# A four-phase decoder trunk: second-layer weights in row-wide pieces, waits for one head's routing, three value slots on VectorE while a chunk is mixed, and the first chunk alone ahead of the first gather

## The reference, cut to what matters

```python
def peer(xn, w_q, sub_keys, u_tab, v_tab):
    q = (xt @ w_q).reshape(t, PEER_HEADS, 2, PEER_HALF)
    s = jnp.einsum("thpd,hpnd->thpn", q, sub_keys)
    # two top-16 lists per head, their 256 sums, top 16 of these -> idx, softmax g
    u = jnp.take(u_tab, ic, axis=0)
    a = jnp.einsum("cd,chkd->chk", xc, u)
    w = gc * jax.nn.gelu(a, approximate=False)
    vv = jnp.take(v_tab, ic, axis=0)
    return jnp.einsum("chk,chkd->cd", w, vv)
```

## Time and profile before

| | |
|---|---|
| median of 3 runs | 1624.27 us |
| the profiled execution's own time | 1625.22 us |
| its span, first to last instruction | 1623.3 us |
| busy share PE / DVE / ACT / POOL | 83% / 66% / 29% / 62% |
| bytes moved, mean rate | 617.13 MB, 380 GB/s |
| of these gathers / SP's transfers | 536.94 MB / 79.26 MB |
| PE's granted clock, mean | 0.91 of 2.4 GHz |

### The profile page before, as it was taken

How to read it: one execution, slowest core, us unless ns; L and a number is a source line. 1 busy time by engine, 2 the same in 40 slices (tenths; PEclk the granted TensorE clock), 3 DMA queues, 4 the chain that set the end, 5 groups by cost and what they waited for, 6 DMA issues and landing times.

```text
span 1623.3 us, 17094 instructions
## 1 busy us (share of the span) xinstructions
PE 1339.6 (83%) x4558; PEld 769.0 (47%) x4558; DVE 1073.2 (66%) x2529; ACT 468.5 (29%) x1427; POOL 1013.6 (62%) x1099
## 2 busy tenths in 40 slices
PE   7999798888895899888777799989877978777775
PEld 7887544444552564354343376546444433322222
DVE  4248689988775545637787635664877977755555
ACT  0203333333332222432233221441333322211112
POOL 0006677777547655766666745675777677777774
PEclk9999999999997998899989899999988989888887
DMA  9519999999999999999999999999999999999997
GB/s 335 180 57 369 397 396 409 404 405 405 393 389 365 399 391 394 407 406 390 400 402 403 410 392 387 402 392 367 408 401 404 409 410 409 409 409 409 410 409 274
DMA packets 222153, 617.13 MB, mean 380 GB/s; under 512 B 18881, under 2 KB 88571, under 8 KB 222075
## 3 DMA queue, kind: packets, MB, share of 16 engines
q0 software_dynamic: 147456, 536.94, 84.0%
q1 hardware_dynamic: 74619, 79.26, 14.7%
HBM read 615.07 MB, written 1.05 MB: 380 GB/s over the span
## 4 chain that ended last, share of the span: by engine, by line
PE 33%; DMA 20%; POOL 15%; issue 13%; DVE 11%; ACT 6%; POOLq 0%; SPq 0%; DVEq 0%; ACTq 0%
DMA u_ring<-in_peer_u_dram,idx_now 18%; PE acc L807 16%; PE tile L777 13%; POOL v_ring L532 8%; POOL u_ring L532 7%; DVE u_ring L1022 5%; ACT diag L622 2%; ACT gelus L616 2%; DMA v_ring<-in_peer_v_dram,idx_now 2%; PE tile L909 1%; PE xf L777 1%; PE tile L904 1%; DVE xres L1049 0%; ACT pq L718 0%; PE tile L799 0%
## 5 line engine op out<-in xcount | busy, mean ns | idle before, releaser
L807 PE MATMUL acc<-v_ring,diag 128*128 128x512 f32 x1780 | 864.7, 644 | 117.7 <-ACT diag L622 64.8
L1022 DVE CUSTOM_DVE_ANT_0 u_ring<-u_ring,xf 128x1024 f32<-128x1024 f32 x512 | 613.5, 1215 | 275.3 <-DMA u_ring<-in_peer_u_dram,idx_now 273.0
L532 POOL DMA_INDIRECT v_ring<-in_peer_v_dram,idx_now x512 | 497.1, 971 | 291.8 <-PE acc L807 119.8
L807 PEld LDWEIGHTS acc<-v_ring,diag 128*128 128x128 f32 x1780 | 363.0, 209 | 589.3 <-issue 550.6
L532 POOL DMA_INDIRECT u_ring<-in_peer_u_dram,idx_now x512 | 501.2, 979 | 168.7 <-issue 138.9
L608 ACT ACTIVATE gelus<-dots 128x8 f32<-128x8 f32 x64 | 13.4, 209 | 526.4 <-DVE dots L1022 526.4
L622 ACT ACTIVATE diag<-ident,gelus 128x128 f32<-128x128 f32 x448 | 137.8, 388 | 2.1
L777 PE MATMUL tile<-w_ring,fT 128*128 128x256 f32 x480 | 110.3, 383 | 3.7 <-DVE fT L1171 3.7
L777 PEld LDWEIGHTS tile<-w_ring,fT 128*128 128x128 f32 x480 | 92.1, 193 | 27.4 <-issue 12.0
L616 ACT ACTIVATE gelus<-gelus,gates 128x1 f32<-128x1 f32 x512 | 102.1, 281 | 4.1 <-ACT gelus L608 2.3
L726 ACT ACTIVATE gexp<-best,gstat 128x16 f32<-128x16 f32 x32 | 9.8, 307 | 308.3 <-DVE best L1312 308.3
(11 more groups left out here) (170 smaller groups left out, 1046.1 us busy)
## 6 DMA issues: line engine op xcount, KB each, us to landing
w_ring<-in_peer_wq_dram SPq DMA_DIRECT2D x21, 1024.0 KB, 16.4
w_ring<-in_w_out_dram SPq DMA_DIRECT2D x12, 1024.0 KB, 24.0
w_ring<-in_w_kv_dram SPq DMA_DIRECT2D x12, 1024.0 KB, 16.5
u_ring<-in_peer_u_dram,idx_now POOLq DMA_INDIRECT x512, 10.7
v_ring<-in_peer_v_dram,idx_now POOLq DMA_INDIRECT x512, 10.6
w_ring<-in_w_in_b_dram SPq DMA_DIRECT2D x8, 1024.0 KB, 20.8
u_ring<-in_w_in_a_dram SPq DMA_DIRECT2D x4, 1024.0 KB, 12.2
w_ring<-in_w_mem_kv_dram SPq DMA_DIRECT2D x4, 1024.0 KB, 15.3
```

Source lines behind the costliest of these rows:

```text
L532: pool.indirect_dma_start(ring[:, s, :], None, rows_[:, :], bass.IndirectOffsetOnAxis(idx_now[:, column + s:column + s + 1], 0), element_o ...
L807: ins = pe.matmul(acc[:, 512 * n:512 * n + 512], diag[:, par * G + s, :], v_ring[:, s, 512 * n:512 * n + 512], start=(first and s == 0), s ...
L1022: dve.tensor_tensor_reduce(u_ring[:, s, :], u_ring[:, s, :], xf[:, :], 1.0, 0.0, ALU.mult, ALU.add, dots[:, par * G + s:par * G + s + 1])\
```

## The change

It has four parts.

**Wide pieces.** For layer 2, `k`, `v`, `qf` and `out` no longer come as 3, 3, 4 and 4 pieces of 256 columns, but as 4 pieces each of 256 rows with all columns (768 or 1024): runs of 3 KB or 4 KB. `by_depth` on PE opens both output tiles of a step and goes piece by piece; a piece is free again when its products are done (`depth_used`).

**Own-head waits.** `heads_ready` asks for the head alone in phase 1 too. Two routing steps of phase 1 and the memory steps of layer 2 move to later groups: head 6 and 7 from groups 13, 14 to 14, 15, `mem_k` from 12 to 13, `mem_v` to (1,0), `keys` to (1,8).

**Three folds.** In groups 0 to 10 of phases 1 and 2, slots 2, 5 and 7 are folded by DVE and five are summed by PE. The semaphores `v_added` and `v_folded` become one per slot.

**The start.** Chunk 1's normalization goes behind the memory rows, its first `u` product behind `out` of chunk 0, its first `c` product behind the first routing, and the memory queries `in_q` become one step per chunk. `x` of chunk 1 loads later, the first `u` piece lies in `diag`, and the query piece of head 0 (not 1) is the guest in `kv_buf`.

```diff
+FOLDED_MIXING = [2, 5, 7]
+def folded(q):
+    if not isinstance(q, int):
+        return FOLDED
+    ph, g = divmod(q, GROUPS)
+    return FOLDED_MIXING if 1 <= ph <= 2 and g <= 10 else FOLDED
...
-    chunk0 = [*conv(0, "b0"), ("mem_k", 0), *conv(0, "u1"), ("in_q",), ("mem_v", 0), *attn(0, 0), *conv(0, "c1"),
+    chunk0 = [("in_q", 0), ("mem_v", 0), *attn(0, 0), *conv(0, "c1"), *attn(0, 1), *conv(0, "b1"), *attn(0, 2),
...
-    chunk1 = [*conv(1, "b0", "u1", "c1"), *attn(1, 0), *conv(1, "b1"), *attn(1, 1), *conv(1, "u2"), *attn(1, 2, 3)]
+    chunk1 = [*conv(1, "c0", "b0", "u1", "c1"), ("in_q", 1), *attn(1, 0), *conv(1, "b1"), *attn(1, 1),
+              *conv(1, "u2"), *attn(1, 2, 3)]
...
-        side[0, (3, 5, 7, 9, 11, 12, 13, 14)[h]] += [("route", 1, h)]
+        side[0, (3, 5, 7, 9, 11, 12, 14, 15)[h]] += [("route", 1, h)]
...
-        mix[1] += [("norm", c), ("k", c, 0), ("k", c, 1), ("k", c, 2)]
-        mix[2] += [("v", c, 0), ("v", c, 1), ("v", c, 2), ("forget", c)]
-        mix[3] += [("qf", c, 0), ("qf", c, 1), ("qf", c, 2), ("qf", c, 3)]
+        mix[1] += [("norm", c), ("k", c)]
+        mix[2] += [("v", c), ("forget", c)]
+        mix[3] += [("qf", c)]
...
-        mix[8] += attn(ph, 9) + out(ph, 0, 1, 2, 3) + [rms("ffn", ph)]
+        mix[8] += attn(ph, 9) + [("mix_out", ph), rms("ffn", ph)]
...
+            k = 2 * key[2]
+            return w.rearrange("(k p) n -> p k n", p=P)[:, k:k + 2, col:col + width]
...
-            return HEADS * (ph // 2) + (HEADS if ph == 1 else h + 1)
+            return HEADS * (ph // 2) + h + 1
...
+                    before = PIECES[n - NW]
+                    if before in DEPTH_USE:
+                        sp.wait_ge(depth_used, DEPTH_USE[before] + 1)
+                    else:
+                        filled(sp, LAST_USE[before])
...
-                if s in FOLDED:
-                    when(v_folded, GD * q + FOLDED.index(s) + 1 - GD)
-                else:
-                    when(v_added, GP * q + SUMMED.index(s) + 1 - GP)
+                when(slot_used[s], q)
...
+            def by_depth(tiles, src, ready=None):
+                outs = [take(key) for key in tiles]
+                keys, width = wide(tiles[0])[0:2]
+                deep = KD // len(keys)
+                for n, at in enumerate(keys):
+                    piece_landed(pe, at)
...
-                    if s in FOLDED and not (isinstance(q, int) and q == 0):
+                    if not (isinstance(q, int) and q == 0) and s in folded(q - 1):
                         fold(q - 1, 1 - par, (ph - 1 if q_first else ph) % 2, s)
```

More of the change, by code:

```diff
@@ L60, with summed, sums_before @@
 FOLDED = [7]
+FOLDED_MIXING = [2, 5, 7]
 SUMMED = [s for s in range(G) if s not in FOLDED]
-GP, GD = len(SUMMED), len(FOLDED)
+def folded(q):
[3 more added lines that the diff above has]
+    return FOLDED_MIXING if 1 <= ph <= 2 and g <= 10 else FOLDED
+def summed(q):
+    return [s for s in range(G) if s not in folded(q)]
+def sums_before(q):
+    fixed = q if isinstance(q, int) else GROUPS * (PHASES - 1)
+    n = sum(len(summed(i)) for i in range(fixed))
+    return n if isinstance(q, int) else (q - fixed) * len(SUMMED) + n
 PE_LAST = G // 2
@@ L155, with wide @@
 assert sorted(map(str, PE_START)) == sorted(map(str, START))
+def wide(tile):
+    kind = tile[0]
+    if kind == "k":
+        _, c, i = tile
+        return [("wk", c, n) for n in range(4)], CONV, 512 * i, (512, 256)[i], False
+    if kind == "v":
+        _, c, i = tile
+        return [("wv", c, n) for n in range(4)], CONV, CONV // 2 * i, CONV // 2, True
+    if kind == "qf":
+        _, c, i = tile
+        return [("wqf", c, n) for n in range(4)], D, 512 * i, 512, False
+    if kind == "out" and tile[1] >= 2:
+        _, ph, i = tile
+        return [("wout", ph, n) for n in range(4)], D, 512 * i, 512, True
+    return None
 def step_tiles(step):
@@ L176, in step_tiles @@
         return [("nT", step[1], i) for i in range(2)]
-    if kind in ("k", "v", "qf", "out"):
+    if kind in ("k", "v", "qf"):
+        return [(*step, i) for i in range(2)]
+    if kind == "out":
         return [step]
+    if kind == "mix_out":
+        return [("out", step[1], i) for i in range(2)]
     if kind == "forget":
@@ L219, with pieces_of @@
 LAST_ROUTE = {ph: [r for r in ROUTES if r[0] == ph][-1] for ph in range(PHASES)}
+def pieces_of(tile):
+    if wide(tile):
+        return wide(tile)[0]
+    return [piece_of(tile)] if piece_of(tile) else []
 def piece_of(tile):
+    if wide(tile):
+        return None
     kind = tile[0]
@@ L229, in piece_of @@
     if kind == "out":
-        return (kind, 0, tile[2]) if tile[1] < 2 else tile
+        return kind, 0, tile[2]
     if kind == "q":
@@ L1111, in start_norm @@
                         filled(dve, ("fT", ph - 2, 1))
-                    for i in range(4):
+                    for i in range(4 if ph < 2 else 2):
                         emptied(dve, ("out", ph, i))
@@ L1163, in side @@
                     empties(dve.tensor_tensor(part, part, bank(step)[:, 0:PC], ALU.add), step)
+                elif kind == "mix_out":
+                    ph = step[1]
+                    for key in step_tiles(step):
+                        part = xres[:, ph % 2, 512 * key[2]:512 * key[2] + 512]
+                        filled(dve, key)
+                        empties(dve.tensor_tensor(part, part, bank(key)[:, :], ALU.add), key)
                 elif kind == "ffn":
```

197 lines of the change are left out of this document (126 added, 71 removed).

## The result

| | before | after |
|---|---|---|
| median | 1624.45 us (12 runs) | 1628.55 us (12 runs, 1626.81 to 1630.84) |
| ratio after / before | | 1.0023, 95% interval 1.0014 to 1.0031 |
| the profiled execution, its span | 1625.22, 1623.3 us | 1627.66, 1625.9 us |
| bytes, busy share PE / DVE / POOL | 617.13 MB, 83 / 66 / 62% | 617.10 MB, 79 / 69 / 64% |

The forecast was 1613 us (1602 to 1623) with 0.79 on faster. The kernel is slower, by 0.23%. The work of the DMA engines and the turn came near the forecast. The start came out with the other sign, the folds cost several times what was taken for them, and the assumption under the largest part, that the stream stays full whatever the pieces do, was wrong.

The account below looks back on a forecast made before the run. After a start set by PE, the DMA stream was taken to bound the kernel, bytes over rate. Terms -12 (wide pieces), -4 (turn), +3 (start) and +2 (folds) made -11, so 1613 us for the median; own range 1607 to 1619, whole range 1602 to 1623.

Parts of the forecast that it names:

- What bounds the kernel: After the start, time is the sum of bytes over DMA rate, with POOL, DVE and PE fitting inside.
- Wide pieces, -12: Layer-2 weights in 3 or 4 KB runs instead of 1 KB move nearer 410 GB/s: -12 us, bounds 0 and -12.6.
- By depth, 0: PE's layer-2 products taken piece by piece wait only if pieces land late: put at 0 us.
- Rival 5: PE starves on whole steps, each waiting for its last weight piece: +16 us, 1629 us, chance 0.04.
- The turn, -4: From phase 0 to 1, POOL no longer waits for the last head's routing: -4 us, bounds 0 and -5.
- The start, +3: Before the stream opens, the first gather comes earlier but the copy to `xf` later: +3 us, bounds -7 and +5.
- The dry spell: At the start, early fetches land and the queues run dry before the dots begin: 1.6 us of the start's +3.
- Three folds, +2, at most +9.6: In 22 mixing groups, two more DVE folds stretch POOL's descriptor writing: +2 us, bounds -4.2 and +9.6.
- the bound of -4.2: Lower bound of the folds' term: 1060:1143 at 400 instead of 380 GB/s would be 4.2 us shorter.
- Rival 2: The weight run's length doesn't matter, so the -12 term is 0: 1625 us, chance 0.08.
- Rival 3: A fold stops POOL for its full 1.28 us, 2.56 a group in ten groups without weights: 1637 us, chance 0.07.

Follow-up runs that it names:

- e1: The changed kernel with one fold a group everywhere (slot 7) instead of three: 1617.79 us.
- e12: The changed kernel with one fold a group everywhere and the `w_out` pieces alone in runs of 1 KB: 1614.87 us.
- e2: The changed kernel with the same pieces of 256 rows, each row brought in runs of 1 KB, three folds kept: 1629.39 us.
- e7: The changed kernel with `w_out` pieces held back as in e3 and all second-layer rows in runs of 1 KB as in e2: 1635.06 us.
- e3: The changed kernel with each `w_out` piece held until an attention step's scores are done, one in each of groups 4 to 7, three folds kept: 1614.52 us.
- e5: The changed kernel with the old start: chunk 1's normalization, first u product, memory queries and first c product back ahead: 1629.86 us.
- e10: The changed kernel with three folds in groups 0 to 3 alone and one in groups 4 to 10: 1617.19 us.
- e6: The changed kernel with one fold a group everywhere and the `w_out` pieces held back over groups 4 to 7 as in e3: 1620.49 us.

## Why the prediction was wrong, point by point

Forecast and result lie 15 us apart. By the account and e1, an estimate: the wide pieces missed by some 11 (10.4 won, and the 9.5 of idle that stay with one fold lost again), the folds by some 9, and the start gave about 5 back.

- **What bounds the kernel.** "An edit pays only if it ... moves the same bytes at a higher rate" rested on a stream that stays full. It was full in part because the pieces travelled slowly. That was the step that failed: fullness was read as a property of the gathers, and it was one of gathers and weights together. What the runs showed in its place: 19 us of idle in the two mixings, 9.5 of which stay when the folds are taken back (e1), and 7.9 of these go when `w_out` alone is slow again (e12).
- **Wide pieces, -12.** As work, right: -10.4. "It all lies on the path, since the pieces travel in phases 1 and 2, where the stream is full" is wrong. e2 shows the net of the run's length to be 0.8 us as the change stands, and e7 against e3 shows 20.5 where the pieces are held back. The 3 KB runs came out near the value taken: 125 ns a packet, between 138 (three of 1 KB) and 120 (three quarters of 4 KB).
- **By depth, 0.** Right: no wait of PE is put down to `w_ring`, and pieces land in 9.4 to 13.0 us. Rival 5's cause isn't there. But whether the pieces land in time was asked for PE's products and never for POOL's waits, which the slow pieces had hidden.
- **The turn, -4.** Right: POOL's 16.05 us wait (from 474.49, not 474.55) is gone, 408 GB/s from 474 to 498, 4.2 us of idle gone.
- **The start, +3.** Wrong in sign: -1.9 by the account, 1.3 by e5. The first gather came at 108.24, not 110.7, and the copy to `xf` at 126.76, not 130:

```profile
98.79 14.46 PE L865 MATMUL tile<-hT,u_ring 128*128 128x128 f32 x128
113.08 3.74 PE L865 MATMUL tile<-hT,w_ring 128*128 128x128 f32 x32
117.29 1.45 PE L1058 MATMUL tile<-mkT,qT 64*128 64x256 f32 x4 [0.47 <-ACT qT L712]
```

  The products behind the scores start 9.7 us earlier than in the earlier trace rows (98.79 against 108.46), where 7.3 was counted, and the wait for the copied queries is 0.47 us, not 1. The terms were mis-sized on both sides, and the small balance of two large terms took its sign from that. The working was loose as well: its own terms, 3.6 + 3.6 + 1 - 7.3, put the fetch behind the first dot 0.9 us later, not 1.4. The dry spell that was counted came (v waits to 122.78, u to 129.51; 291 GB/s in 118:142), but the bytes of 95:118, 104 GB/s against 1, weigh more.
- **Three folds, +2, at most +9.6.** Undone it gave 10.8, a little past the bound. The step that failed is "fetches in flight cover much of it": in groups 4 to 10 they cover little (e10: 11.4 us for 14 groups, 0.8 a group, where 0.96 was the full price). The price itself was fair: 0.48 from one row, where the 66 fetches of the kernel before that start inside a fold take 0.41 longer in the mean. The spread wasn't looked at (up to 1.05, by where in the fold the fetch starts), nor the other DVE work that stretches a fetch: a group without weights takes 21.95 us, 1.48 over the stream's. That folds can also give, as e6 against e3 has it, was left at the bound of -4.2.
- **The rivals.** Rival 5's time (1629) is nearest, by luck: no wait of PE for a piece is seen. Rival 2's (1625) is near for another reason than it gave: length matters to the work. Rival 3's lock is real, at 1.5 us a group instead of 2.56. No rival had the cause that e2, e3, e7 and e12 show, a transfer that was useful because it was slow.

The Trainium skill ("SBUF — State Buffer", section "SBUF: two separate sides") speaks of an exclusive lock, held for the whole instruction by a DVE operation with two SBUF inputs against a GpSimd operation that reads SBUF. The fold agrees (0.90 us of the 1.02 that were left of it), and so does the row with 0.48: 0.61 us were left there, so it spoke for the rule and not against it. The dots have two SBUF inputs as well and stretch nothing here, so the rule as worded is too wide for this kernel.

**What stays open.** In every version over 3 us of idle are left in at least one mixing. The length of POOL's wait is followed back to the dots for one wait of phase 1 alone (e12). In phase 2 the same step shows (the last dot at 1006.43 in e1, at 1002.22 in e12), but PE's sums come 6.2 us earlier, more than these 4.2; the rest was not taken apart. No version with more v slots, which might take the wait itself away, was run. e3 (1614.5) and e12 (1614.9) can't be told apart; both beat the kernel before by 0.7%.

## What to carry to other kernels

A full stream is full of something: before making a filler faster, list the waits of the main stream's issuer and ask which transfers stand behind them at that moment. Low-priority loads are worth most in flight during those waits, so try when they are let go as a setting of its own, apart from when a buffer is free: here holding them back was worth 14 us with three folds and cost 2.7 with one. Price a lock from many rows, by where in the holder's run the victim starts, and ask for each stretch whether anything covers the price.

## What the runs showed of the hardware that was not expected

A fold on DVE (`scalar_tensor_tensor`, 128x1024, 1.28 us) holds a fetch's descriptor writing on POOL for a little less than its remaining time (0.94 us alone; 1.42, 1.74 and 1.84 when started 0.67, 0.35 and 0.26 us into a fold; up to 1.97 in the trace of the changed kernel), while the dot-product instruction over the same shapes (1.22 us) doesn't (0.97 at most in 412 fetches that start inside one). And slower transfers beside gathers can make the whole faster: with `w_out` in 1 KB runs instead of 4 KB the DMA engines had 3.4 us more work, and the kernel was 2.9 us quicker (e1, e12).
